# A transformer layer on one core: compress stage moved into the projection's last tile, memory values as the stationary operand, gathered rows turned in four banks

## The chip, the cores and the metric

One core of one Trainium2 chip runs the whole program in one launch; the other cores are idle. The metric is the device time of one execution in microseconds (us). Everything is float32. The program has its weights in DRAM and its tiles in the core's SBUF; products and transposes by TensorE (PE) end in PSUM, which has eight banks of 128 partitions by 512 float32. VectorE (DVE), ScalarE (ACT) and GpSimd (POOL) work beside it, and SyncE (SP) issues most of the transfers. Engines wait for one another on semaphores.

## The reference, cut to what matters

A layer for 1024 tokens (S) of width 1024: projection, two kinds of attention, cross-attention to a memory of 256 tokens, and 32 experts of which each token takes four. Three parts of it are touched.

```python
# compress: blocks of 32 tokens, stride 16 (63 blocks), for k and for v, two groups g
blk = t[:, cmp_idx] + pos_emb[None, None, :, None, :]
hid = jax.nn.gelu(jnp.einsum('bnlgd,ldf->bngf', blk, w1))      # l 32, d 64, f 128
out = jnp.einsum('bngf,fd->bngd', hid, w2)                     # k's is RMS-normed behind it

# memory attention: 4 heads of 64, 256 memory rows
s = jnp.einsum('bqhd,bkhd->bhqk', q, k) * MEM_HD ** -0.5
p = jax.nn.softmax(s, axis=-1)
o = jnp.einsum('bhqk,bkhd->bqhd', p, v).reshape(B, S, 256)
x = x + o @ w_mo

# experts, top 4 of 32
gu  = t[tok] @ w_gate_up[e] + b_gate_up[e]                     # 1024 -> 2048
act = (up + 1.0) * gate * jax.nn.sigmoid(1.702 * gate)         # clamped gate and up
y   = act @ w_down[e] + b_down[e]                              # 1024 -> 1024, times the gate weight
```

## The kernel before, in words

`program` (L1915) runs the stages one after the other, with a barrier of all engines between two: setup, memory, project, compress, attend, mix, experts. Setup writes a table of relative biases; memory computes the keys and values of the 256 memory rows (`kTm` with heads on two row halves, `vmem`).

**Project** (`stage_project`, L208) goes through eight tiles of 128 tokens, written out as a software pipeline: in tile t TensorE does the products `into(t + 1, ...)` of the next tile in pieces, and between them the steps of tile t: `turn_c` (transposes, L451), `up`, `turn_n` (eight transposes: normed queries and keys, and the raw columns that compress needs), `turn_q` (sixteen transposes of 96 columns' worth of heads, L479). In the last tile, t = 7, no next products stand between these steps. ACT and VectorE copy each turned bank to SBUF, and SP stores it to DRAM (`d_qm`, `d_km` at L282 are the last); the compress columns are stored to the SBUF tile `cnT` by a DMA. At SP's top stands the copy of the bias table to `d_bias` (`rev_copied`). In tile 7 SP also issues `load_compress` (L520 to L527), ten loads of `w1`, `w2` and the position embeddings into the place of `w_in`, whose last product is over.

**Compress** (`stage_compress`, L530): TensorE turns the position embeddings (they become 32 more columns of `cnT`), then does the products at L573, 64 for each of k and v and each group, all with 64 rows of contraction, group 0 on row half 0 and group 1 on row half 1, alternating, into a bank each. ACT computes gelu, TensorE the second product, VectorE and ACT the norm of k, TensorE turns k, SP stores `d_ck` and `d_cv` (L558). At its start SP issues `load_first` (L632): the identity, queries, keys and values of the first head pair, the mask strip and `cvalid`.

**Attend** (`stage_attend`, L643) works through 4 head pairs of 32 units; a unit's scores, maximum (L901), exponential (L859, ACT), transposes (L793) and values follow one another over the engines with two units in flight. VectorE waits at its top for POOL's memset of the score tile `sc` (L709) and for `first_in`; SP's first loads are those of the first pair's other tables (L724), and the gates at the end, which VectorE needs at L939.

**Mix** (`stage_mix`, L1047) has eleven steps; in step t TensorE works on tile a = t (output projection), b (memory queries and scores, L1427), c (memory softmax and values, L1414, output product) and d (router, expert biases by the gates, L1439). The list of TensorE's instructions is written out by hand, and so is VectorE's. For tile c: the probabilities `pr` are turned (eight transposes), then each head's values come from two products with the turned probabilities stationary and 64 moving columns of `vmem` (L1414); VectorE scales the result by the softmax sums to `o` (L1306), TensorE turns `o` in two transposes, VectorE copies `oT` (L1325), and the output product follows. For tile d: `gm`, the gate weights by expert, is turned to `gmT` (32 rows), and two products with 512 columns of `bdown` add the biases (L1439).

**Experts** (`stage_experts`, L1455) is a loop of passes, 32 of which do work, each with one expert and up to 256 rows. The pass's number of rows, read from a plan in DRAM, decides through `ARMS` which segments it has: f of 128 rows in four units, h of 64 in two, q of 32, g of 64; "a block" below is segment f. A pass on TensorE: the gate-up products (L1788) unit by unit; the turning of the activations (`turn_act`, L1766); the turning of the *next* pass's gathered rows `xg` (`turn_rows`, L1756 to L1762: four row banks' worth of two columns each, 8 transposes for one block of rows, 16 for two); then the down products (`whole` at L1878, `half` at L1893), in whose second chunk `last_turn` turns the last activations. ACT copies the turned rows, `copy_rows` (L1587) to `xT_e`, and the turned activations (L1607) to `aT`, in one order: the activation copies of this pass come before the row copies. The row banks are two, `ROW_BANK = (7, 5)`, used twice each, so turn k waits for the copy of turn k - 2.

```python
for k in range(4):
    pe.wait_ge(s_xTc, CREDIT + 4 * i + max(k - 1, 0))
    for kk in range(2):
        for b in range(nb):
            c = 2 * k + kk
            mm = pe.transpose(ps[:, ROW_BANK[k % 2], kk * PASS + b * P:kk * PASS + (b + 1) * P], xg[:, b, c * P:(c + 1) * P], ident[:, :])
    mm.then_inc(s_xT, 1)
```

## Time and profile before

| what | value |
|---|---|
| median of 3 runs (lowest, highest) | 3097.82 us (3090.96, 3100.35) |
| the profiled execution's own time | 3101.04 us |
| its span in the trace | 3099.3 us |
| mean granted TensorE clock | 0.944 of full |
| TensorE busy | 2753.2 us (89%), 12040 instructions |
| VectorE, ScalarE, GpSimd busy | 1121.5 (36%), 592.7 (19%), 220.3 (7%) |
| transfers | 570.19 MB, mean 184 GB/s |
| gate-up products (L1788) | 1032.2 us |
| down products (L1878) | 531.6 us |
| one VectorE operation on 128x1024 from PSUM (L1733) | 1.28 us |

In the rows below a group or instruction is named by its engine, its line in the program, its operation and `out<-in` by the names of the tiles; then come shapes and a count. In brackets or behind the last bar stands the idle time of the engine just before it, and behind `<-` what released it (engine, tile, line). "issue" means that nothing the profile shows was waited for. SPq and POOLq are the instructions with which these engines issue transfers. PEclk is the clock that TensorE was granted, as a share of full speed. Stages in this execution: projection to about 350 us, compress to 391, attention to about 880, mix to 1196, experts to the end.

### The profile page before, as it was taken

How to read it: one execution, taken by the hardware profiler on the slowest of the kernel's cores; microseconds unless marked ns; L12 is line 12 of the kernel's file. 1: busy time of each engine (PE TensorE's matmuls, PEld its weight loads, DVE VectorE, ACT ScalarE, POOL GpSimd, SP SyncE). 2: the span in 40 equal slices, each digit the busy share in tenths (PEclk: the TensorE clock that was granted, in tenths of full speed). 3: DMA queues.
4: the chain of work that ended last, by engine and by line, in shares of the span. 5: the costliest groups of instructions: out<-in, count | busy, mean ns of one | idle time of the engine just before them, and what ended most of it. 6: DMA issues, size and time to landing. Idle time of an engine off the chain costs nothing.

```text
span 3099.3 us, 41426 instructions
## 1 busy us (share of the span) xinstructions
PE 2753.2 (89%) x12040; PEld 1369.3 (44%) x12041; DVE 1121.5 (36%) x2925; ACT 592.7 (19%) x1582; POOL 220.3 (7%) x188
## 2 busy tenths in 40 slices
PE   6999589999879984899999899999999999899995
PEld 3555456666545652343444344434333434344332
DVE  2667357767636652223222121221222222122221
ACT  1222145655523320000000000000001000010000
POOL 0000000000001111100000100010110010100110
PEclk9999689999989975899999999999999999999998
DMA  8322562130031205957556777587887677755880
GB/s 291 88 60 61 123 184 53 41 92 15 15 96 48 69 28 213 362 186 261 179 184 226 295 288 271 181 286 266 299 312 254 249 261 248 299 183 182 295 303 14
DMA packets 294613, 570.19 MB, mean 184 GB/s; under 512 B 78734, under 2 KB 117646, under 8 KB 274040
## 3 DMA queue, kind: packets, MB, share of 16 engines
q1 hardware_dynamic: 255661, 530.27, 48.0%
q0 software_dynamic: 21152, 38.52, 5.4%
q10 hardware_dynamic: 17707, 0.22, 0.3%
q8 instruction: 52, 0.85, 0.1%
q14 instruction: 41, 0.34, 0.0%
HBM read 542.65 MB, written 69.88 MB: 198 GB/s over the span
## 4 chain that ended last, share of the span: by engine, by line
PE 49%; DMA 5%; issue 3%; DVE 2%; ACTq 1%; ACT 1%; POOL 0%; POOLq 0%; SPq 0%; DVEq 0%
PE ps L1788 27%; PE ps L1878 17%; DMA out<-ys_e,dst 3%; PE ps L1893 2%; PE ps L1761 1%; DVE gu L1689 1%; DMA xg<-d_h,src 1%; PE ps L1766 1%; DMA wg<-in_w_gate_up 1%; ACT xT_e L1587 1%; ACTq L1502 0%; DVE gg L1692 0%; DVE ys_e L1733 0%; POOL out L1569 0%; DVE ys_e L1731 0%
## 5 line engine op out<-in xcount | busy, mean ns | idle before, releaser
L1788 PE MATMUL ps<-wg,xT_e 128*64 128x512 f32 (+2 forms) x4032 | 1032.2, 599 | 35.9 <-issue 26.5
L1788 PEld LDWEIGHTS ps<-wg,xT_e 128*64 128x64 f32 (+2 forms) x4032 | 390.1, 146 | 647.4 <-issue 647.4
L1878 PE MATMUL ps<-w_rows,aT 128*128 128x512 f32 x1152 | 531.6, 617 | 9.1 <-ACT xT_e L1587 9.1
L1689 DVE TENSOR_TENSOR gu<-ps,bias 64x512 f32<-64x512 f32 (+2 forms) x252 | 173.6, 689 | 587.9 <-PE ps L1788 561.5
L1878 PEld LDWEIGHTS ps<-w_rows,aT 128*128 128x128 f32 x1152 | 222.5, 198 | 273.4 <-issue 271.4
L1629 ACT ACTIVATE ss<-gg 128x256 f32<-128x256 f32 x146 | 60.8, 416 | 1374.6 <-issue 763.3
L1733 DVE TENSOR_SCALAR ys_e<-ps,dst 128x1024 f32<-128x1024 f32 x36 | 46.2, 1284 | 579.8 <-PE ps L1878 579.8
L1569 POOL DMA_INDIRECT out<-ys_e,dst x64 | 101.9, 1592 | 1408.9 <-DVE ys_e L1733 926.2
L442 PE MATMUL ps<-w_in,hT_a 128*128 128x430 f32 x512 | 193.4, 530 | 6.3 <-DVE hT_a L345 6.3
L793 PE MATMUL ps<-ident_t,sc 128*128 128x128 f32 x880 | 151.8, 290 | 29.7 <-ACT sc L859 26.2
L859 ACT ACTIVATE sc<-sc,nm 128x640 f32<-128x640 f32 (+15 forms) x256 | 161.5, 633 | 54.0 <-DVE nm L901 54.0
L1761 PE MATMUL ps<-ident_e,xg 128*128 128x128 f32 x392 | 63.2, 304 | 92.3 <-ACT xT_e L1587 54.7
L793 PEld LDWEIGHTS ps<-ident_t,sc 128*128 128x128 f32 x880 | 97.3, 142 | 90.5 <-ACT sc L859 63.2
L442 PEld LDWEIGHTS ps<-w_in,hT_a 128*128 128x128 f32 x512 | 95.8, 192 | 88.0 <-issue 79.6
L1699 DVE TENSOR_TENSOR aa<-vv,ss 128x256 f32<-128x256 f32 x146 | 62.1, 425 | 155.9 <-ACT ss L1629 145.8
L1362 PE MATMUL ps<-w_rows,yT_x 128*128 128x512 f32 x256 | 114.6, 602 | 1.4 <-DVE yT_x L1218 1.4
L908 DVE COPY pT<-ps 128x512 f32<-128x512 f32 (+3 forms) x176 | 86.0, 488 | 72.8 <-PE ps L793 72.0
L1607 ACT ACTIVATE aT<-ps 128x256 f32<-128x256 f32 x146 | 52.2, 376 | 278.7 <-PE ps L1766 274.2
L852 ACT ACTIVATE pT<-ps 128x512 f32<-128x512 f32 (+3 forms) x176 | 76.2, 433 | 133.8 <-PE ps L793 133.3
L1761 PEld LDWEIGHTS ps<-ident_e,xg 128*128 128x128 f32 x392 | 48.4, 155 | 103.6 <-ACT xT_e L1587 62.7
L1554 POOL DMA_INDIRECT xg<-d_h,src x66 | 68.6, 1039 | 296.0 <-issue 296.0
L1766 PEld LDWEIGHTS ps<-ident_e,aa 128*128 128x128 f32 x292 | 50.6, 200 | 78.3 <-issue 58.7
(293 smaller groups left out, 2473.7 us busy)
## 6 DMA issues: line engine op xcount, KB each, us to landing
wg<-in_w_gate_up SPq DMA_DIRECT2D x128, 2048.0 KB, 9.1
w_rows<-in_w_down SPq DMA_DIRECT2D x128, 1024.0 KB
bias<-in_b_gate_up SPq DMA_DIRECT2D x32, 1024.0 KB, 9.4
d_bias<-d_rev SPq DMA_DIRECT2D x1, 10368.0 KB, 38.1
w_in<-in_w_in SPq DMA_DIRECT2D x1, 6880.0 KB, 24.8
x_a<-in_x POOLq DMA_DIRECT2D x8, 512.0 KB, 4.2
kn<-d_kn SPq DMA_DIRECT2D x8, 512.0 KB
strip_t<-d_bias SPq DMA_DIRECT2D x8, 512.0 KB
```

Of the source, the lines that this page charges most:

```text
L442: mm = pe.matmul(ps[:, 4 * b + c, 0:PCH], hT[b][:, k, :], w_in[:, k, c * PCH:(c + 1) * PCH], start=(k == 0), stop=(k == KD - 1))
L793: mm = pe.transpose(ps[:, 4 + h, (i % 4) * P:(i % 4 + 1) * P], sc[:, u % DEPTH, h, i * P:(i + 1) * P], ident[:, :])
L852: act.activation(dst, src, ACT.Copy).then_inc(s_cp[h], 1)
L859: act.activation(sc[:, k, h, 0:w], sc[:, k, h, 0:w], ACT.Exp, bias=nm[:, k, h, n - 1:n], scale=-1.0, accum_out=rs[:, k, h:h + 1]).then_inc ...
L908: dve.tensor_copy(dst, src).then_inc(s_cp[h], 1)
L1362: mm = pe.matmul(ps[:, bank, 0:cols.stop - cols.start], src[:, k, :], w[:, k, cols], start=(k == 0), stop=(k == n - 1))
L1569: pool.indirect_dma_start(out=e.out[0], out_offset=bass.IndirectOffsetOnAxis(ap=dst[:, b, 0:1], axis=0), in_=ys[:, b, :], in_offset=None, ...
L1689: read = dve.tensor_tensor(gu[part, :], ps[part, BANK[k][j], :], bias[part, cols], ALU.add)
L1761: mm = pe.transpose(ps[:, ROW_BANK[k % 2], kk * PASS + b * P:kk * PASS + (b + 1) * P], xg[:, b, c * P:(c + 1) * P], ident[:, :])
L1766: mm = pe.transpose(ps[:, ACT_BANK[k][j], f * P:(f + 1) * P], aa[:, AA[k][j], f::2], ident[:, :])
L1788: mm = pe.matmul(ps[g * kind:(g + 1) * kind, BANK[k][j], :], xT[:, kk, t0:t0 + kind], wg[:, j * groups + g, kk, :], start=(kk == 0), stop= ...
L1878: mm = pe.matmul(ps[:, 2 + 2 * b + h, :], aT[:, j, b * P:(b + 1) * P], wd[:, c, j % 2, h * 512:(h + 1) * 512], start=(j == 0), stop=(j == ...
```

## The change

Three parts. **Front:** `stage_compress` is gone and its work is in tile 7 of the projection. The position embeddings are loaded at SP's top; `turn_last` turns them and the raw columns straight to a bank that ACT copies to `cnT` (the two transposes in `turn_n` and the store to `cnT` go in this tile); k's 128 products and the first quarter of v's stand before `turn_q`, the rest behind it, with the second products. k's loads and v's have a semaphore each. `load_first` (identity, mask strip, `cvalid`) is issued in tile 1, the first pair's queries, keys and values (`load_first_heads`) at the end of the projection, into the place of the last three of the eight row groups of `w_in`, a tile of its own now. In attention the memset of `sc` is gone, and the first values wait for `first_v_in`. **Mix:** the probabilities are scaled before they are turned, `vmem` is the stationary operand with two heads on two column halves, so that the product comes out turned and `o`, its two transposes and their copy go; the gate weights are doubled, and the two bias products use row groups 0 to 31 and 32 to 63. **Experts:** four row banks, no wait between the turns, the wait for the row copies at other places.

```diff
-N_MEMORY, N_PROJECT = 5, 14
+N_MEMORY, N_PROJECT = 5, 15
...
-    for dst, src in ((e.ident_a[:, :], e.c_ident), (e.w_in_t[:, :, :], e.w_in[0].rearrange("(k p) n -> p k n", p=P)),
+    w_in = e.w_in[0].rearrange("(k p) n -> p k n", p=P)
+    for dst, src in ((e.ident_a[:, :], e.c_ident), (e.w_in_t[:, :, :], w_in[:, 0:KD - 3, :]), (e.w_in_end[:, :, :], w_in[:, KD - 3:, :]),
```

SP in the projection:

```diff
+                    if t == 1:
+                        load_first(nc, e, sp)
                     if t == NT - 1:
                         load_compress(nc, e, sp)
...
+                sp.wait_ge(s_kT, 1)
+                sp.dma_start(e.d_ck.rearrange("g d n -> d g n"), kT[:, :, :]).then_inc(s_out, 16)
+                sp.wait_ge(s_cc, 1)
+                sp.dma_start(e.d_cv.rearrange("g n d -> n g d"), cc[:, G:, :]).then_inc(s_out, 16)
                 for b in range(2):
-                    sp.wait_ge(s_st[b], 160 * (NT // 2))
+                    sp.wait_ge(s_st[b], 160 * (NT // 2) - 16 * b)
+                load_first_heads(e, sp)
+                sp.wait_ge(s_out, 32)
```

TensorE in the projection:

```diff
+                def turn_last():
...
+                    for i in range(2):
+                        at = i * (P + CMP_LEN)
+                        pe.transpose(ps[:, 0, at:at + P], pr[b][:, C_KC + i * P:C_KC + (i + 1) * P], ident[:, :])
+                        mm = pe.transpose(ps[:, 0, at + P:at + P + CMP_LEN], pos[:, i, :, :].rearrange("p g d -> p (g d)"), ident[0:CMP_LEN, 0:CMP_LEN])
+                    mm.then_inc(s_last, 1)
+
+                def products(i, ls):
+                    if ls[0] == 0:
+                        pe.wait_ge(e.cmp_in[i], 16 * N_CMP)
+                        pe.wait_ge(s_cnT, 1)
...
+                    for l in ls:
+                        for g in range(G):
+                            half = slice(g * HD, (g + 1) * HD)
+                            mm = pe.matmul(ps[:, CMP_BANK[i][g], 0:NCMP + 2], w1[half, i, l, :], e.cnT[half, i, l:l + S + 1:CMP_STRIDE],
+                                           start=(l == 0), stop=(l == CMP_LEN - 1))
...
+                    if not more:
+                        turn_last()
                     turn_c(t)
...
+                    else:
+                        products(0, range(CMP_LEN))
+                        products(1, range(CMP_LEN // 4))
                     turn_q(t)
...
+                second(0)
+                products(1, range(CMP_LEN // 4, CMP_LEN))
+                pe.wait_ge(s_ck, 1)
...
+                second(1)
```

Attention:

```diff
-                pool.memset(sc[:, :, :, :], 0.0).then_inc(s_set, 1)
...
+                    if u == 0:
+                        pe.wait_ge(e.first_v_in, 32)
...
-                dve.wait_ge(s_set, 1)
-                dve.wait_ge(e.first_in, 16 * N_FIRST_MLA)
+                dve.wait_ge(e.strip_in, 48)
```

Mix, VectorE:

```diff
+                        wait("p", c, MH)
+                        step(dve.reciprocal(rs[:, c, :], rs[:, c, :]))
+                        dve.tensor_tensor(pr[:, :, :], pr[:, :, :], bcast(rs[:, c, :].unsqueeze(2), [P, MH, N_MEM]), ALU.mult).then_inc(m["pn"], 1)
...
-                        dve.tensor_tensor(o[:, :, :], ps[:, 6, 0:256].rearrange("p (h d) -> p h d", d=MHD),
-                                          bcast(rs[:, c, :].unsqueeze(2), [P, MH, MHD]), ALU.mult).then_inc(m["on"], 1)
+                        dve.tensor_copy(oT[:, :, :], ps[:, 6, 0:256].rearrange("p (j n) -> p j n", n=P)).then_inc(m["oTd"], 1)
```

Mix, TensorE:

```diff
-                        for j in range(2 * MH):
-                            mm = pe.matmul(ps[:, 6, (j // 2) * MHD:(j // 2 + 1) * MHD], pT[:, j, :], e.vmem[:, j % 2, j // 2, :], start=(j % 2 == 0), stop=(j % 2 == 1))
+                        for pair in range(MH // 2):
+                            for k in range(2):
+                                for h in range(2):
+                                    j = 2 * pair + h
+                                    mm = pe.matmul(ps[h * MHD:(h + 1) * MHD, 6, pair * P:(pair + 1) * P], e.vmem[:, k, j, :], pT[:, 2 * j + k, :], start=(k == 0), stop=(k == 1))
...
-                            mm = pe.matmul(ps[:, 2 + c2, :], gmT[:, :], bdown[:, c2 * 512:(c2 + 1) * 512], start=True, stop=True)
+                            r = slice(c2 * NE, (c2 + 1) * NE)
+                            mm = pe.matmul(ps[:, 2 + c2, :], gmT[r, :], bdown[r, :], start=True, stop=True)
```

Experts:

```diff
-        ROW_BANK = (7, 5)
+        ROW_BANK = (7, 4, 5, 0)
...
-                        pe.wait_ge(s_xTc, CREDIT + 4 * i + max(k - 1, 0))
...
+                        pe.wait_ge(s_aTc["g"], CREDIT + 2 * i + 2)
+                        hold(pe, e.pe_passed)
                         with pe.If(after > P):
                             turn_rows(i + 1, 2)
```

`last_turn`, `whole` and `half` of the experts:

```diff
-                            rows_copied(3)
+                            rows_copied(1)
...
                             if b:
-                                rows_copied(4)
-                                copied("g", 2)
+                                rows_copied(3)
                                 copied("h", 1)
                             else:
-                                copied("f", 3)
+                                for k, have in (("q", 1), ("h", 1), ("f", 3)):
+                                    copied(k, have)
...
+                            rows_copied(2)
                             copied(*(("h", 1) if turn else ("q", 1)))
```

## Rows read from the trace of the kernel before

**Rows 1.** Page, the chain that ended last, shares of the span by engine.
```profile
PE 49%; DMA 5%; issue 3%; DVE 2%; ACTq 1%; ACT 1%; POOL 0%; POOLq 0%; SPq 0%; DVEq 0%
```
**Rows 2.** Groups by line, 1200 to 3099 us: busy us, mean ns | idle before.
```profile
L1761 PE MATMUL ps<-ident_e,xg 128*128 128x128 f32 x392 | 63.2, 304 | 92.3 <-ACT xT_e L1587 54.7 <-DMA xg<-d_h,src 37.6
```
**Rows 3.** TensorE in order of time, one pass: start us, us, what, [idle before].
```profile
1709.44 0.60 PE L1761 MATMUL ps<-ident_e,xg 128*128 128x128 f32 x4
1711.82 0.66 PE L1761 MATMUL ps<-ident_e,xg 128*128 128x128 f32 x4 [1.77 <-ACT xT_e L1587]
1712.36 5.39 PE L1878 MATMUL ps<-w_rows,aT 128*128 128x512 f32 x8
```
**Rows 4.** ACT in order of time, same pass.
```profile
1710.55 0.64 ACT L1607 ACTIVATE aT<-ps 128x256 f32<-128x256 f32 x2
```
**Rows 5.** TensorE in order of time, a pass without a block.
```profile
2198.66 6.78 PE L1878 MATMUL ps<-w_rows,aT 128*128 128x512 f32 x8 [1.11 <-ACT xT_e L1587]
```
**Rows 6.** Windows in experts: us, busy of PE PEld DVE ACT POOL, clock, DMA, GB/s.
```profile
1360.50:1364.00 3.50, 3.50 (x10) 1.62 (x9) 0.00 (x0) 0.49 (x2) 0.00 (x0) 1.00 1.05 408
1712.40:1717.60 5.20, 5.20 (x10) 2.17 (x10) 0.00 (x0) 0.45 (x2) 0.00 (x0) 0.67 1.06 422
2198.70:2205.30 6.60, 6.60 (x9) 2.74 (x10) 0.00 (x0) 0.00 (x0) 0.00 (x0) 0.53 1.05 410
```
**Rows 7.** TensorE in order of time, end of projection and compress.
```profile
320.54 0.90 PE L451 MATMUL ps<-ident_a,cn 128*128 128x128 f32 x3 [7.01 <-DVE cn L370]
...
341.32 3.54 PE L479 MATMUL ps<-ident_a,qk 128*96 128x128 f32 x16 [9.91 <-DVE qk L408]
...
356.69 27.57 PE L573 MATMUL ps<-cnT,w_in 64*128 64x65 f32 x256 [0.32 <-DVE cnT L606]
```
**Rows 8.** SP's issues in order of time, 329 to 394 us.
```profile
329.35 4.47 SPq L527 DMA_DIRECT2D w_in<-in_cmp_v_w  x1
...
346.58 0.54 SPq L282 DMA_DIRECT2D d_km<-qkT  x1
...
390.80 0.52 SPq L558 DMA_DIRECT2D d_cv<-cc  x1
...
393.38 0.33 SPq L724 DMA_DIRECT2D qn<-d_qn  x1
```
**Rows 9.** Transfers by issue: KB each, median us from issue to landing.
```profile
d_bias<-d_rev SPq DMA_DIRECT2D x1, 10368.0 KB, 38.1
...
w_in<-in_cmp_v_w SPq DMA_DIRECT2D x1, 32.0 KB, 9.9
```
**Rows 10.** Windows, columns as in rows 6: projection's last tile, compress, mix.
```profile
330.00:332.00 2.00, 1.07 (x8) 0.86 (x8) 1.93 (x4) 0.20 (x1) 0.00 (x0) 1.00 1.22 204
356.70:384.20 27.50, 27.50 (x257) 27.38 (x257) 0.16 (x1) 0.52 (x2) 0.00 (x0) 0.50 0.35 79
1104.00:1119.00 15.00, 9.21 (x65) 8.07 (x63) 11.02 (x26) 4.70 (x8) 0.00 (x0) 1.00 0.18 70
```
**Rows 11.** Attention's start in order of time; last, km's issue to landing.
```profile
393.38 6.92 POOL L709 MEMSET sc<- 128x8192 f32 x1 [117.39 <-POOLq L98]
...
402.36 1.15 ACT L859 ACTIVATE sc<-sc,nm 128x1024 f32<-128x1024 f32 x1 [7.69 <-DVE nm L901]
...
411.25 0.23 DVE L939 TENSOR_SCALAR gates<-gates,cvalid 128x8 f32<-128x8 f32 x1 [2.66 <-DMA gates<-d_gt]
...
DMA to landing us min/median/max: 8.3/8.6/8.8
```
**Rows 12.** Mix: TensorE's groups by line, 1000 to 1100; VectorE in order of time.
```profile
L1439 PE MATMUL ps<-bdown,gmT 32*128 32x512 f32 x15 | 7.4, 608 | 0.0
L1414 PE MATMUL ps<-vmem,pT_x 128*128 128x64 f32 x48 | 5.7, 272 | 0.0
L1427 PE MATMUL ps<-kTm,qT_x 64*128 64x256 f32 x24 | 3.4, 402 | 0.0
...
1020.71 0.19 DVE L1276 TENSOR_TENSOR lg<-ps,rb 128x32 f32<-128x32 f32 x1 [5.57 <-PE ps L1362]
```

More of the change, by code:

```diff
@@ L236, in stage_project @@
         nT = pair("nT", [P, 8, P])
+        pos = sb("pos_c", [CMP_LEN, 2, G, HD])
+        pb = sb("pb", [CMP_HID, 2])
+        hid = sb("hid", [CMP_HID, 2, G * NCMP])
+        cc = sb("cc", [NCMP, 2 * G, HD])
+        sqc = sb("sq_c", [NCMP, G, HD])
+        stc = sb("st_c", [NCMP, G])
+        kT = sb("kT_c", [HD, G, NCMP])
         names = lambda *ns: (e.dma_sem("a_" + n) for n in ns)
@@ L323, in _ @@
                         spread(t + 2)
+                    if t == NT - 1:
+                        act.wait_ge(s_last, 1)
+                        act.activation(e.cnT[:, :, t * P:], ps[:, 0, 0:2 * (P + CMP_LEN)].rearrange("p (i n) -> p i n", i=2), ACT.Copy).then_inc(s_cnT, 1)
                     rest(t)
+                act.wait_ge(s_ssqc, 1)
+                act.activation(stc[:, :], stc[:, :], ACT.Sqrt, bias=eps[0:NCMP, 0:1], scale=1.0 / HD).then_inc(s_stdc, 1)
+                hidden(1)
             @block.vector
```

246 lines of the change are left out of this document (103 added, 143 removed).

## The prediction

> **What bounds the kernel now.** Read the page first: TensorE is busy 89% of the span (the table above), and the chain that ended last is half TensorE, most of it the experts' two lines of products (L1788, L1878) [rows 1]. So I ask where TensorE stands still, and go through the stages in which the change has a part: the experts (1200 to 3099 us), the end of the projection and the compress stage behind it (313 to 411 us), the mix stage (880 to 1196 us).
>
> *Experts.* In the groups of lines, L1761, the turning of the next pass's rows, has the largest idle time before it: 54.7 us until ACT has copied a bank, 37.6 us until a gather lands [rows 2]. The order of time shows the first within one pass: four transposes, 1.77 us idle until ACT's copy of the first row bank, four more, then the down products at once [rows 3]. ACT was late for a second reason: before the row copies it did the activation copies of the same pass, which ended at 1711.19 [rows 4]. Passes without a block of 128 rows also wait 1.11 us for the fourth copy before their down products [rows 5]. And the clock: behind such a gap the first eight down products (3.5 us at full clock) took 5.2 and 6.6 us, at a granted clock of 0.67 and 0.53 [rows 6]. Of the 32 passes, eleven show this: five of 5.3 us, six of 5.4 to 6.8 us, together 24 us over 3.6.
>
> *Projection to attention.* The last tile leaves TensorE idle until 320.5 and from 331.4 to 341.3; behind it the compress stage runs alone: 256 instructions of products in 27.57 us [rows 7]. SP's issues mark the ends: last projection store 346.58, the compress stage's last store 390.80, attention's first load 393.38 [rows 8].
>
> **The change, part by part.** Times are from the profiled execution (span 3099.3, its own time 3101.04, 3.2 above the median 3097.82).
>
> 1. *Rows turned in four banks.* No transpose waits for a copy. With one block of rows the eight take 8 x 0.15 = 1.2 us [rows 3]. The first down products now wait for the activation copies instead (explicit waits for q, h and f): in the pass of [rows 3, 4] start 1711.19 + 0.06, against 1712.36, so 1.1 us saved of 1.77 idle. With two blocks the 16 transposes (2.4 us) are the longer term. Done for every pass by its own rows: 20 passes with a 128-row block save 0.87 to 1.46, 23.1 us; nine without it must still have three row copies, 0.28 us each for one block and 0.55 for two, behind the activation copies, and save 11.3 us; the three small ones save 2.4 us (two of them begin with a late gather). Sum 37 us. The new wait for g's two copies costs at most 0.3 us in the one pass that has g; elsewhere the count is there long before. The last turn's wait is for the row bank it uses and comes 3.5 us later: nothing. The gather chain starts at the end of the previous pass's down products, and the saving lies before that point, so it isn't lost to it.
>    Clock: the stretch without large products shrinks from 3.0 to 1.9 us in block passes and from 5 to about 4 us in the others. I take back the five smaller falls (8.4 us) and 3 us of the 15.7 of the others, since in those the gate-up weights, issued at the end of the units, land only a few us before the next pass. Bounds: 0 and 24 us; taken 11. **Experts 48 us**, bounds 30 and 61.
>
> 2. *Compress in the last tile.* turn_last (four transposes) fits into the idle time before 320.5, and ACT's added copy (some 0.5 us) too: there ACT waits for VectorE as TensorE does. k's products start at 331.4. v's last load was issued at 329.35 and lands 9.9 us later, at 339.3 [rows 8, 9]; the pos loads are gone from between, so no later. 16 pairs of v, 1.7 us, end at 341.0. turn_q at full clock, 16 times 0.15 less overlap, 2.2 us, 343.5; the two evictions and stores follow, 1 us before today's. ACT does k's hidden units in between (2 us with their table load, an estimate), done at 340.7. second(0), 0.7 us, and 48 pairs, 5.2 us: 349.4. Then today's tail without its key half (which runs beside the pairs: root, scale and turning done by 350.2): hidden 0.7, product 0.5, copy 0.3: d_cv issued at 351.3. Four loads of the first heads behind it on SP, 3 us, and 1 us of barrier: attention begins at 355.8 against 393.38, 37.6 us earlier.
>    What is late next: before, scores began at once and VectorE waited for the memset, so that the first exponential stood 9.0 us into the stage [rows 11]. Now km, issued at 352.3, lands 8.6 us later [rows 11], 360.9, and I give scores and maximum 7.1 us (before, both fitted into less than those 9.0): the exponential 12.2 us into the stage. VectorE then stops at the gates, which landed 17.9 us into the stage [rows 11] at the end of SP's first loads; 2 MB of first-head loads lie ahead of them in the same queue, 4 to 8 us at the 200 to 250 GB/s of these stretches, of which 3 are over before the stage. I take 5.3 us given back. **Front 32 us**. The clock is the open term: at 0.50 throughout k ends at 345.2, the 16 pairs at 348.6, turn_q at 352.1, the rest at 362.8, attention at 369.4, which leaves 19 us. I take the full clock, since the nearest row has low work holding it: 15 us of transposes and narrow products, TensorE 61% busy, at 1.00, though the 27.5 us of products never raised it from 0.50 [rows 10]. The memset's 6.92 us are no extra gain: 2.66 of waiting for the gates hid behind them.
>    A rule against the trace: the rows show TensorE busy for all of 27.5 us and the clock at 0.50 to the end. The Trainium skill (TensorE: Matmul & The Clock Gate, "Why this matters for your kernels") says that sustained busy time brings the full rate; by it the old products would have risen too and cost some 15 us, and the gain would be about 13 us smaller. The trace disagrees for these narrow products, and the sum goes by the rows.
>
> 3. *Mix stage*, where TensorE is the bound in the steady tiles: no idle time before its product groups [rows 12]. Per tile: the value products take 0.119 us per instruction [rows 12], 16 of them 1.9; with the 64-column values stationary on two column halves, two at a time, I take 0.055, 0.9. Two transposes go, 0.15 each as in [rows 3], 0.3 us, with the round trip over VectorE. The bias products, 0.49 us each [rows 12], four in a row; kTm's of 256 columns on two row halves take 0.14 each where one after the other would give twice that [rows 12], so the two biases side by side save 0.86. Sum 2.2, less 0.1. Added on VectorE: the scaling of 1024 probabilities (1.28 us for as many columns in the table above) and a copy; it has 5.57 us idle there before the logits [rows 12] and its product is wanted 4 us later: nothing. Eight tiles: **17 us**. Lower bound, if nothing runs side by side: 5; upper 21.
>
> Moving 0.5 MB of strip and two small loads to tile 1 and splitting w_in are hidden: SP awaits d_bias's copy, which is issued before the first tile and lands 38.1 us later [rows 9], before tile 1's stores are due, and what SP stores there is awaited two tiles later.
>
> Sum 48 + 32 + 17 = 97: 3101.0 - 97 = 3004 on the profiled execution, **3001** as a median.
>
> **The rivals.** (a) *Half clock in the products*: for it, they never raised it; against, the 15 us at 1.00. It costs 13 us: 3014. (b) *The experts' wait only changes hands*: ACT's activation copies and row copies set the start of the down products anyway, or the weights, and the clock falls as before. For it, 1.1 saved of 1.77; against, weights issued 20 us ahead in passes with a block. Experts 30: 3019. 
> **How the numbers follow.** What a measurement of this kernel can tell is 0.3%, 9 us. Forecast 0.50, (a) 0.18, (b) 0.16, (c) 0.05, (d) 0.06, (e) 0.03, a race of several small losses that ends within 0.3% 0.02. (a) and (b) together give 3032. Range 2980 to 3035. Faster 0.95, same 0.02, slower 0.03.
>
> **What would show it.** Right: idle before the rows' transposes only from gathers, about 38 us; the first eight down products 3.6 us in nearly all passes; attention's first load near 356; clock 1.00 from 331 to 349; the mix period 2.1 us shorter. Wrong: products at 0.215 a pair, turn_q behind 345; a wait for v's weights of over 1 us; TensorE idle before the down products by more than 0.7 us; the wait for the gates over 6 us.

## The result, and the profile after

The changed kernel takes 3014.05 us (median of 4 runs, 3010.69 to 3017.63) against 3097.72 for the kernel before (4 runs): ratio 0.973, 95% interval 0.9718 to 0.9743, or 84 us less. The forecast was 3001 with a range of 2980 to 3035. On the profiled executions, against which the sum was made, the span goes from 3099.3 to 3012.1: 87.2 us where 97 were forecast.

Five points in the order of time cut the span into stages: the issue of attention's first load, the end of its last value product, the start of the last expert count of mix (L1418), the start of the first gate-up product, the end of the last down product.

| us | before | after | gained | forecast |
|---|---|---|---|---|
| start to attention's first load | 393.4 | 358.5 | 34.9 | 37.6 |
| attention, to its last value product | 451.7 | 459.2 | -7.5 | -5.3 |
| mix, to the last expert count | 336.1 | 320.0 | 16.1 | 17 |
| to the first gate-up product | 41.5 | 43.3 | -1.8 | 0 |
| experts, to the last down product | 1845.1 | 1799.0 | 46.1 | 48 |

This table compares one execution with one. Experiment 1 shows how far each stage moves by itself, and two of these gains change by it: experts (36 us instead of 46) and mix (near 19 instead of 16).

**Experts.** Part 5 of the page after, the groups that answer to [rows 2], and the page before's down products (which had 531.6 busy and 9.1 idle):

```profile
L1798 PE MATMUL ps<-wg,xT_e 128*64 128x512 f32 (+2 forms) x4032 | 1033.3, 601 | 40.6 <-issue 27.9
L1890 PE MATMUL ps<-w_rows,aT 128*128 128x512 f32 x1152 | 515.0, 602 | 31.2 <-ACT xT_e L1598 18.9
L1771 PE MATMUL ps<-ident_e,xg 128*128 128x128 f32 x392 | 53.6, 291 | 42.1 <-DMA xg<-d_h,src 40.3
L1906 PE MATMUL ps<-w_rows,aT 128*64 128x512 f32 x352 | 82.4, 616 | 3.1 <-ACT xT_e L1598 3.1
```

The 54.7 us in which the row transposes waited for ACT are gone; what is left before L1771 are gathers, but for 1.8 us. A part stands before the down products now: 31.2 us, against 9.1. From the end of the last activation transposes to the first down product the 32 passes took 131.1 us in sum before and 95.6 after. TensorE in order of time, a pass with one block of rows and one without a block, and ACT in the first of them:

```profile
2034.18 1.04 PE L1771 MATMUL ps<-ident_e,xg 128*128 128x128 f32 x8
2036.24 1.12 PE L1890 MATMUL ps<-w_rows,aT 128*128 128x512 f32 x2 [1.03 <-ACT aT L1618]
...
2126.53 1.04 PE L1771 MATMUL ps<-ident_e,xg 128*128 128x128 f32 x8
2130.42 5.23 PE L1890 MATMUL ps<-w_rows,aT 128*128 128x512 f32 x8 [2.86 <-ACT xT_e L1598]
```

```profile
2034.97 0.42 ACT L1640 ACTIVATE ss<-gg 128x256 f32<-128x256 f32 x1 [6.41 <-DVE gg L1703]
2035.29 0.64 ACT L1618 ACTIVATE aT<-ps 128x256 f32<-128x256 f32 x2
```

The start of the down products is now ACT's: it does a sigmoid (L1640) before the activation copies and these before the rows. The clock: the first eight down products took 3.5 us (from the first to the next other instruction) in nearly every pass, and over 5 in 4 of them (11 before), 118.1 us in sum against 136.2. The four are all passes without a block, and the length of the stretch does not tell which: with 4.12 and with 4.32 us between the last activation transposes and the down products, one pass of each had the fall and another had not.

**Front.** TensorE in order of time after (L562 are the compress products, L538 is `turn_q`, L570 the second products, L790 attention's first scores), and windows as in [rows 6, 10]:

```profile
329.19 7.50 PE L562 MATMUL ps<-cnT,w_in 64*128 64x65 f32 x128
338.61 3.68 PE L562 MATMUL ps<-cnT,w_in 64*128 64x65 f32 x32 [1.91 <-DMA w_in<-in_cmp_v_w]
342.22 3.27 PE L538 MATMUL ps<-ident_a,qk 128*96 128x128 f32 x16
345.41 0.44 PE L570 MATMUL ps<-w_in,hid 128*63 128x64 f32 x4
345.79 5.69 PE L562 MATMUL ps<-cnT,w_in 64*128 64x65 f32 x96
...
363.82 7.03 PE L790 MATMUL ps<-w_in_end 96*128 96x512 f32 x12 [11.10 <-DMA w_in_end<-d_km]
```

```profile
329.20:336.60 7.40, 7.40 (x129) 7.30 (x128) 6.89 (x6) 2.51 (x4) 0.00 (x0) 1.00 1.23 212
338.70:342.20 3.50, 3.50 (x32) 3.40 (x32) 0.64 (x2) 0.04 (x1) 0.00 (x0) 0.50 0.30 76
345.80:351.20 5.40, 5.40 (x97) 5.40 (x97) 2.42 (x7) 3.60 (x4) 0.00 (x0) 1.00 0.56 144
363.80:370.80 7.00, 6.97 (x12) 3.13 (x12) 2.93 (x9) 0.84 (x1) 0.00 (x0) 0.64 0.99 242
```

k's 128 instructions ran at full clock, 0.117 us a pair; the 27.57 us of [rows 7] have become 16.87, and of these only a part is not hidden. v's first quarter waited 1.91 us for its load and then ran at 0.50, and `turn_q` behind it took 3.27 us. SP's issues after, and VectorE at the gates:

```profile
353.07 0.27 SPq L303 DMA_DIRECT2D d_cv<-cc  x1
...
358.51 4.55 SPq L735 DMA_DIRECT2D qn<-d_qn  x1
...
375.11 0.41 SPq L745 DMA_DIRECT2D gates<-d_gt  x1
```

```profile
380.92 0.23 DVE L951 TENSOR_SCALAR gates<-gates,cvalid 128x8 f32<-128x8 f32 x1 [5.65 <-DMA gates<-d_gt]
```

VectorE works on the gates 22.4 us into the stage; before it was 17.9 [rows 11].

**Mix.** Groups of lines with shapes apart, TensorE, before (880 to 1180 us) and then after (852 to 1137 us); both windows hold 28 of the 32 bias instructions:

```profile
L1362 PE MATMUL ps<-w_mo,oT_x 128*128 128x512 f32 x64 | 34.2, 684 | 1.9 <-DVE oT_x L1325 1.5
L1414 PE MATMUL ps<-vmem,pT_x 128*128 128x64 f32 x128 | 17.7, 299 | 3.9 <-DVE pT_x L1217 3.9
L1439 PE MATMUL ps<-bdown,gmT 32*128 32x512 f32 x28 | 17.4, 751 | 0.4 <-DVE gmT L1312 0.4
L1432 PE MATMUL ps<-ident_x,o_x 128*128 128x128 f32 x16 | 4.0, 335 | 0.0
```

```profile
L1429 PE MATMUL ps<-pT_x,vmem 128*64 128x128 f32 x128 | 10.5, 316 | 2.7 <-DVE pT_x L1229 2.7
L1450 PE MATMUL ps<-bdown,gmT 32*128 32x512 f32 x28 | 9.8, 782 | 0.8 <-DVE gmT L1327 0.8
```

Both pairs run side by side: 17.7 us of value products became 10.5, and 17.4 us of bias products 9.8.

### The profile page after: what moved, and what is told of

It is laid out like the page before. It is cut to its first block, busy times and chain, and to the rows that moved or that the text cites. A ratio compares the mean times of both kernels' runs of the same rounds, so it can differ in the third digit from the quotient of the medians.

```text
span 3012.1 us, 41358 instructions
## 1 busy us (share of the span) xinstructions
PE 2702.6 (90%) x12024; PEld 1344.0 (45%) x12025; DVE 1129.3 (37%) x2931; ACT 589.9 (20%) x1585; POOL 219.0 (7%) x187
## 4 chain that ended last, share of the span: by engine, by line
PE 47%; DMA 7%; issue 3%; DVE 2%; ACTq 1%; ACT 1%; POOL 0%; POOLq 0%; SPq 0%; DVEq 0%
PE ps L1798 26%; PE ps L1890 16%; DMA out<-ys_e,dst 4%; PE ps L1906 2%; DMA xg<-d_h,src 1%; DMA wg<-in_w_gate_up 1%; PE ps L1771 1%; PE ps L1776 1%; DVE gu L1700 1%; ACTq L1513 0%; DVE ys_e L1744 0%; POOL out L1580 0%; ACT aT L1618 0%; DVE gg L1703 0%; DVE ys_e L1742 0%
## 5 line engine op out<-in xcount | busy, mean ns | idle before, releaser
L1798 PE MATMUL ps<-wg,xT_e 128*64 128x512 f32 (+2 forms) x4032 | 1033.3, 601 | 40.6 <-issue 27.9
L1890 PE MATMUL ps<-w_rows,aT 128*128 128x512 f32 x1152 | 515.0, 602 | 31.2 <-ACT xT_e L1598 18.9
L1640 ACT ACTIVATE ss<-gg 128x256 f32<-128x256 f32 x146 | 60.8, 417 | 1383.6 <-issue 775.4
L804 PE MATMUL ps<-ident_t,sc 128*128 128x128 f32 x880 | 151.6, 289 | 30.1 <-ACT sc L872 26.7
L501 PE MATMUL ps<-w_in,hT_a 128*128 128x430 f32 x320 | 128.1, 538 | 6.3 <-DVE hT_a L386 6.3
L865 ACT ACTIVATE pT<-ps 128x512 f32<-128x512 f32 (+3 forms) x176 | 76.1, 433 | 135.0 <-PE ps L804 134.5
L1771 PE MATMUL ps<-ident_e,xg 128*128 128x128 f32 x392 | 53.6, 291 | 42.1 <-DMA xg<-d_h,src 40.3
L1906 PE MATMUL ps<-w_rows,aT 128*64 128x512 f32 x352 | 82.4, 616 | 3.1 <-ACT xT_e L1598 3.1
L501 PEld LDWEIGHTS ps<-w_in,hT_a 128*128 128x128 f32 x320 | 59.9, 195 | 54.7 <-issue 46.4
```

The lines of the kernel that those rows point to most:

```text
L501: mm = pe.matmul(ps[:, 4 * b + c, 0:PCH], hT[b][:, k, :], w_in_rows(k)[:, c * PCH:(c + 1) * PCH], start=(k == 0), stop=(k == KD - 1))
L804: mm = pe.transpose(ps[:, 4 + h, (i % 4) * P:(i % 4 + 1) * P], sc[:, u % DEPTH, h, i * P:(i + 1) * P], ident[:, :])
L1771: mm = pe.transpose(ps[:, ROW_BANK[k], kk * PASS + b * P:kk * PASS + (b + 1) * P], xg[:, b, c * P:(c + 1) * P], ident[:, :])
L1798: mm = pe.matmul(ps[g * kind:(g + 1) * kind, BANK[k][j], :], xT[:, kk, t0:t0 + kind], wg[:, j * groups + g, kk, :], start=(kk == 0), stop= ...
L1890: mm = pe.matmul(ps[:, 2 + 2 * b + h, :], aT[:, j, b * P:(b + 1) * P], wd[:, c, j % 2, h * 512:(h + 1) * 512], start=(j == 0), stop=(j == ...
L1906: mm = pe.matmul(ps[h * r:(h + 1) * r, 4, :], aT[:, j, t0:t0 + r], wd[:, c, j % 2, h * 512:(h + 1) * 512], start=(j == 0), stop=(j == JD - 1))
```

## The experiments

Twelve kernels. Each ratio is to the kernel before, run beside it; a median is compared with the changed kernel's 3014.05 us where the edit is on the changed kernel.

**1. The parts alone.** Each is the kernel before with one part of the diff shown above, cut at the stages.

> The kernel before with the experts' part alone. Theory: the three parts are separate stages and add up, so this one brings what the experts' stage gained between the two traces, 46 us (35.5 of waits before the down products, some 17 of clock, 6 given back to the gate-up weights): about 3051 us, ratio 0.985. Rival (it only pays in a kernel in which the stages before are also shorter, or weights and gathers take it back): under 30 us, 3068 or more. Rival (two thirds of the whole gain is here): 60 us or more, 3038.

> The kernel before with the mix part alone. Theory: TensorE is the bound of that stage, 16.2 us between the traces (about 2.1 per step): 3081.5 us, ratio 0.9948. Rival (the shorter products only expose VectorE, the gain between the traces came from another alignment): under 8 us. The 1.5 us that the experts' start lost would be seen here too, if it belongs to this part.

> The kernel before with the front part alone. Theory: attention's first load stands 35 us earlier, of which attention's start gives back 7.5 (gates later in the queue, half clock behind the idle time): 27.5 us, 3070 us, ratio 0.991. My forecast had 32 (3066). Rival (the memset that is gone hides more, or the barrier is shorter): over 32.

Measured: experts 3060.40, ratio 0.9876 (0.986 to 0.9891), some 38 us; mix 3077.11, 0.9927 (0.9912 to 0.9941), 23 us; front 3071.11, 0.9908 (0.9893 to 0.9922), 28 us. The sum is 89, and together they bring 84, within what these intervals allow: the parts add up. The stages in the traces, us:

| kernel | to attention's first load | attention | mix | granted clock in mix | experts |
|---|---|---|---|---|---|
| before | 393.4 | 451.7 | 336.1 | 0.888 | 1845.1 |
| experts alone | 391.0 | 452.4 | 338.8 | 0.878 | 1808.4 |
| mix alone | 391.0 | 452.4 | 320.1 | 0.876 | 1843.3 |
| front alone | 356.9 | 458.2 | 338.7 | 0.878 | 1838.1 |
| all | 358.5 | 459.2 | 320.0 | 0.876 | 1799.0 |

How far a stage moves by itself is seen where a kernel does not touch it. The old experts' stage stands in five traces (before, mix alone, front alone and the two of experiment 2): 1829.1 to 1845.1 us, 1839.4 on average. The new one stands unchanged in five (experts alone, all, experiments 6, 7 and 8): 1799.0 to 1810.8, 1803.4 on average. So the part is worth some 36 us in the traces and 38 in the runs; the 46 between the two profiled executions of the table above came from a long one before and a short one after. The averages of the terms: from activation transposes to down products 130.4 us before and 95.9 after; first eight down products 135.0 and 121.3 (9 to 12 falls, then 4 to 7); waits for gate-up weights 6.9 and 12.6; waits of the activation transposes for VectorE 10.8 and 14.3.

Mix moves with the granted clock. At nearly the same clock the part is worth 18.7 us (338.8 against 320.1); the 336.1 of the kernel before was an execution with a higher clock in that stage.

**2. Mix in halves**, on the kernel before. Values alone is the mix part with these lines, and the tiles `gm` and `gmT` that belong to them, put back; bias alone is the kernel before with these lines the other way, the gate weights doubled.

```diff
-bdown = sb("bdown", [2 * NE, D // 2])
+bdown = sb("bdown", [NE, D])
...
-                            r = slice(c2 * NE, (c2 + 1) * NE)
-                            mm = pe.matmul(ps[:, 2 + c2, :], gmT[r, :], bdown[r, :], start=True, stop=True)
+                            mm = pe.matmul(ps[:, 2 + c2, :], gmT[:, :], bdown[:, c2 * 512:(c2 + 1) * 512], start=True, stop=True)
```

> The kernel before with the values part of the mix change alone (probabilities scaled first, values stationary on two column halves, no turning of o). Theory: my forecast's terms, 1.0 for the products and 0.3 for the transposes a tile, less what VectorE's scaling adds: mix stage about 10 us shorter (336 to 326), 8 tiles. Rival (the scaling of 1024 columns, 1.22 us, delays the transposes of the probabilities and takes part of it back): 6 or less.

> The kernel before with the bias part alone (gate weights doubled, two products on two row groups). Theory: the two run side by side, 1.0 us saved a tile less the copy: mix stage 6 to 8 us shorter. Rival (they run one after the other, or the copy on VectorE sits on the path): under 3 us. Values and bias together should make the 16 to 17 us that the mix part makes alone.

Values alone: 3086.91, ratio 0.997 (0.9955 to 0.9984), stage 325.7 at a granted clock of 0.885, so 10.4 us shorter than the 336.1 at 0.888, as expected. Bias alone: 3093.27, 0.9985 (0.9975 to 0.9995), stage 336.3 at a granted clock of 0.876, so 2.5 us less than the 338.8 of the kernels with the old mix at nearly that clock (0.878), where 6 to 8 were expected; the runs differ by 3.4. Yet its products did halve. Groups of lines, bias alone:

```profile
L1363 PE MATMUL ps<-w_mo,oT_x 128*128 128x512 f32 x64 | 33.8, 677 | 6.2 <-DVE oT_x L1326 6.2
L1441 PE MATMUL ps<-bdown,gmT 32*128 32x512 f32 x28 | 9.8, 781 | 0.4 <-DVE gmT L1313 0.4
```

In TensorE's list the bias products stand between the turning of `o` and the output product, which waits for VectorE's copy `oT`. They covered that copy; made short, they expose it: 6.2 us of waiting, 1.9 before. Over the stage TensorE is busy 7.2 us less than with the old mix in those kernels (278.4 against 285.6) and idle 5.2 us more (58.1 against 52.9). Once the values part has taken `o`'s turning away, the bias part brings 7.5 us: 325.7 with values alone at a clock of 0.885, and 318.2 with the whole part at 0.886 (experiments 6 and 8).

**3. All row copies awaited** before the down products, on the changed kernel.

```diff
+                            rows_copied(4)
                             if b:
-                                rows_copied(3)
...
-                            rows_copied(2)
+                            rows_copied(4)
```

> The changed kernel, but the down products wait for all four row copies in every pass. The idle time before the down products grows: with a block of rows by the copies behind the activation copies, 1.0 us (one block) or 2.0 us (two blocks) in some 21 passes, by 0.2 to 0.5 in nine others: waits 30 to 35 us. Theory of the clock (it falls where the stretch without large products is over some 3.5 us, as in the 11 passes before): stretches grow to 3 to 4 us, so some of the 27 passes that hold it now lose it, 1.7 us each: 3014 + 33 + 5 to 25 = 3050 to 3070. Rival (the clock follows something else than that stretch, and does not fall): 3045. Rival (the waits are covered by the gate-up weights, which land later anyway): under 3035.

Measured 3074.46, ratio 0.9923 (0.9904 to 0.9942), 60 us slower than the change, and the experts' stage is 1859.9 us, longer than before the change. From the activation transposes to the down products 139.6 us (44 more than with the change), and 17 passes with a clock fall instead of 4, 142.0 us for the first eight products (24 more). Both terms of the theory were right in kind and low in size: the stretch grew by more than the 30 to 35 us expected, the clock took the top of 5 to 25, and the time lies above 3050 to 3070. But the length that the expectation names for a fall is not in the rows. Counted from the last gate-up product to the first down product, five of the eleven falls before stood behind 3.2 to 3.3 us, and eight passes with 3.7 to 4.2 us had none; here, of two passes with 3.67 us one fell. What decides in one pass stays open.

```profile
L1890 PE MATMUL ps<-w_rows,aT 128*128 128x512 f32 x1152 | 536.9, 622 | 68.6 <-ACT xT_e L1598 68.6
```

**4. Wide products in the wait**, on the changed kernel.

```diff
                             whole(0, ("f", 3))
                         with pe.Else():
+                            for _ in range(3):
+                                pe.matmul(ps[:, 6, :], ident[:, :], wide[:, :], start=True, stop=True)
```

`wide` is a tile of zeros, set by POOL at the start of the stage.

> The changed kernel with three products of 512 columns (six instructions, 2.6 us at full clock) between the turned rows and the down products in the nine passes without a block, where TensorE waits 2.0 to 2.9 us for the row copies. What they compute is not used, and the wait itself stays. Theory of the clock (it falls because nothing large runs in that stretch, whatever the reason): the four falls among these passes go, up to 7 us of the experts' stage, and waits are unchanged within 3 us: stage 1792 to 1797 against 1799. Rival (the fall comes from the transposes or from the transfers then running, not from the missing products): four or more falls stay, and the stage is the same or longer.

Measured 3018.57, ratio 0.9748 (0.973 to 0.9765). No fall is left, the first eight products take 107.6 us in sum against 118.1. In order of time, the pass that is shown above:

```profile
2127.53 1.04 PE L1774 MATMUL ps<-ident_e,xg 128*128 128x128 f32 x8
2128.40 2.74 PE L1918 MATMUL ps<-wide,ident_e 128*128 128x512 f32 x6
2131.42 3.70 PE L1894 MATMUL ps<-w_rows,aT 128*128 128x512 f32 x8 [0.27 <-ACT xT_e L1601]
```

From the last row transpose to the down products it is 2.85 us as before, and the eight products take 3.70 instead of 5.23. So the fall comes from the stretch without large products, not from the transposes or the transfers beside it. The runs do not tell this kernel from the changed one. Its stage is 8 us longer in the trace (1807.2), where 2 to 7 less was expected. The stretches before the down products add 13 us, partly in two of the three small passes, where the products had no wait to fill, and the clock gives 10.5 back; gate-up weights are waited for 18.9 us instead of 11.2. The untouched stage moves by 12 us, so the 8 are not told from nothing, but a gain is not there either.

**5. ACT's order**, on the changed kernel.

```diff
                                 for j in range(4):
+                                    if j == 3:
+                                        copy_act(i, "f", 2)
                                     sigmoid("f", j)
-                                    if j:
+                                    if j in (1, 2):
                                         copy_act(i, "f", j - 1)
...
                             with act.Else():
                                 none("f")
...
+                                sigmoid("h", 0)
+                                with act.If(hasq > 0):
+                                    copy_act(i, "q", 0)
                                 copy_act(i, "h", 0)
...
+                                next_rows(i + 1, after)
+                                sigmoid("h", 1)
                                 copy_act(i, "h", 1)
```

> The changed kernel with another order on ACT: with a block of rows, the copy of the block's third turned activation comes before the sigmoid of its fourth; without a block, the activation copies and the row copies come before the sigmoid of h's second half. Theory (ACT's order sets the start of the down products, and the clock goes with the length of the stretch without large products): some 15 waits of 1.0 us before the down products go and nine of 2.4 to 2.9 shrink to under 0.7, together 30 us, and the four clock falls go, 7 us; the gate-up weights take back 6 to 12: 3014 - 28 = 2986. Rival (the gate-up weights and the gathers, not ACT, set the pass's length from here on): under 10 us gained, 3005 or more, with the waits moved before the gate-up products. Rival (the sigmoid that is now late holds up the last turned activation by as much): TensorE waits before the last turn of a pass, and nothing is gained.

Measured 2992.99, ratio 0.9659 (0.964 to 0.9677), 21 us faster than the change. Its experts, two of the groups of lines from 1175 to 3060:

```profile
L1901 PE MATMUL ps<-w_rows,aT 128*128 128x512 f32 x1152 | 507.4, 595 | 13.9 <-ACT aT L1618 7.9 <-ACT xT_e L1598 6.0
L1809 PE MATMUL ps<-wg,xT_e 128*32 128x512 f32 x1280 | 150.7, 625 | 33.7 <-DMA wg<-in_w_gate_up 31.9 <-issue 1.8
```

Down to 68.9 us between activation transposes and down products (26.7 less), no clock fall, 8.4 us less for the first products. And the rival's part: the wait for gate-up weights is 31.9 us in the passes' narrow segment, 11.2 with the change and 7.5 before. The gate-up products themselves take 10.5 us longer (1043.8 against 1033.3). Of some 35 us won before and in the down products the stage keeps 12 in this trace (1787.0), which is the slowest of its five runs; the medians keep 21. The weights' wait is the same in the second kernel with this order (32.6 us, experiment 9). What the next step meets are the weights.

**6. The gates first**, on the changed kernel: their load moved from the end of SP's first tables to the front.

```diff
-                    if hp == 0:
-                        sp.dma_start(gates[:, :, :, :], e.d_gt.rearrange("(t p) (h b) -> p t h b", p=P, b=3)).then_inc(s_gate, 16)
...
+                sp.dma_start(gates[:, :, :, :], e.d_gt.rearrange("(t p) (h b) -> p t h b", p=P, b=3)).then_inc(s_gate, 16)
                 load_nsa(0)
                 load_mla(1)
```

> The changed kernel with the load of the gates as the first of attention's loads. Theory: VectorE's wait of 5.65 us for them goes, and attention's give-back of 7.5 us against the kernel before shrinks to about 3: 3014 - 4 = 3010. Rival (the rest of the first tables, or the scores at half clock, are as late): less than 1.5 us. Below what the runs can tell; the stage's length in the trace decides it.

Measured 3007.77, ratio 0.9717 (0.9695 to 0.974): the intervals overlap with the change's, so the trace decides. VectorE no longer waits at the gates. From the stage's first load (356.9) to its last value product it takes 451.1 us, 8.1 less than with the change, twice the 4 expected, and as long as before. In six traces with the changed attention as it is the stage takes 456.8 to 460.1, so the 8 stand clear of its own movement: the give-back of 7.5 hung on this one load.

**7. Wide products before the first scores**, on the changed kernel.

```diff
                 pe.wait_ge(e.strip_in, 48)
+                for _ in range(20):
+                    pe.matmul(ps[:, 5, :], ident[:, :], mstrip[:, 0:512], start=True, stop=True)
                 scores(0)
```

> The changed kernel with 20 products of 512 columns into an unused bank at the start of attention, while TensorE waits for the first queries and keys. What it computes is not used. Theory (the idle time of 11 us is why the first twelve scores run at a granted clock of 0.64 and 7.0 us instead of some 4.7): clock 1.00 from the first score, the first exponential 2 to 3 us earlier, attention 2 to 4 us shorter: 3011. Rival (the gates' wait swallows what the scores gain): attention's length unchanged within 1 us. Rival (the products last longer than the wait for the keys): some us slower.

Measured 3019.68, ratio 0.9747 (0.9727 to 0.9767). The intervals of this kernel and the changed one overlap. The products ran 19.2 us (two instructions each; I had reckoned with one) and ended some 12 us after the scores had begun with the change. Their windows, and the scores behind them:

```profile
350.00:356.70 6.70, 0.45 (x5) 0.34 (x5) 0.28 (x1) 0.34 (x3) 0.00 (x0) 0.76 0.66 161
356.70:359.00 2.30, 2.30 (x3) 1.14 (x4) 0.00 (x0) 1.24 (x1) 0.00 (x0) 0.50 1.01 227
359.00:362.00 3.00, 3.00 (x6) 1.14 (x5) 0.00 (x0) 0.00 (x0) 0.00 (x0) 0.78 1.32 202
362.00:366.00 4.00, 4.00 (x11) 1.84 (x10) 0.00 (x0) 0.00 (x0) 0.00 (x0) 1.00 1.05 250
...
375.80:380.00 4.20, 4.20 (x13) 2.02 (x11) 2.79 (x7) 0.69 (x1) 0.00 (x0) 1.00 1.04 226
```

At full clock the twelve score instructions take 4.46 us, not 7.03. They began 11.9 us later than with the change, and VectorE came to the gates 3.6 us later (384.54 against 380.92) without a wait: 11.9 less the 2.6 of clock and less the 5.65 of waiting. So the scores had room up to the gates' wait. The stage is 462.1 us long, 2.9 more than with the change, where 2 to 4 less was expected.

**8. k's products wait for v's load too**, on the changed kernel.

```diff
-                        pe.wait_ge(e.cmp_in[i], 16 * N_CMP)
+                        pe.wait_ge(e.cmp_in[0], 16 * N_CMP)
+                        pe.wait_ge(e.cmp_in[1], 16 * N_CMP)
```

> The changed kernel, but k's products too wait for v's loads. Theory: k's 128 products start when v's load lands, 338.6 instead of 329.2, v's first quarter and the turning of the last queries move by the 9.4 us less the 1.9 us that they wait today, and attention's first load comes 7.5 us later, 3021. Rival (the end of the stage hangs on ACT's and VectorE's tail of the projection, so that k's products have slack): under 3 us, 3016. If the clock falls in the longer idle time (half clock in the products): 7 us more.

Measured 3024.93, ratio 0.9765 (0.9744 to 0.9787), 11 us slower than the change. In order of time, then windows on these products, on `turn_q` and on the rest of v's products:

```profile
338.00 17.33 PE L563 MATMUL ps<-cnT,w_in 64*128 64x65 f32 x160 [7.28 <-issue]
```

```profile
341.00:355.00 14.00, 14.00 (x136) 14.00 (x134) 0.00 (x0) 1.97 (x4) 0.00 (x0) 0.50 0.01 1
355.30:358.30 3.00, 3.00 (x17) 2.78 (x16) 0.00 (x0) 0.00 (x0) 0.00 (x0) 0.58 0.00 0
358.80:364.00 5.20, 5.20 (x93) 5.20 (x94) 2.37 (x7) 3.56 (x4) 0.00 (x0) 1.00 0.57 145
```

Attention's first load stands at 370.8, 12.3 us later. Behind 7.28 us of idle time the products ran at half clock to their end, 0.217 us a pair: the forecast's rival (a), made to happen by one wait. The separate waits are worth 12 us in the trace and 11 in the runs, more by the clock (some 8 us for these 160 instructions) than by the start.

**9. Together**: ACT's order, the gates first, and five wide products before the scores (ten instructions).

> The changed kernel with the other order on ACT, the gates loaded first, and five products of 512 columns (10 instructions, some 6.5 us with the clock rising) ahead of attention's first scores. Theory (separate stages, gains add): experts' stage 1787 us as with the order alone, attention 8 to 10 us shorter by the gates and 1 to 3 by the clock: 2993 - 10 = 2983, ratio 0.963. Rival (with the gates first, the first loads end later and the products only push the scores back): 2990 or more.

Measured 2987.84, ratio 0.9647 (0.9628 to 0.9667): 26 us below the changed kernel and 109 below the one before, the fastest here. Most of it is ACT's order; the interval does not tell it from that kernel alone, but the trace does: attention ends its value products at 808.2, against 816.7 there. The scores run at a granted clock of 1.00 and take 4.46 us, the first exponential stands 9.9 us into the stage instead of 11.7 with the gates alone, and the stage is 449.7 us long against 451.1. That is the 1 to 3 us expected of the wide products, but no more than the stage moves by itself, so it is not shown.

## Why the prediction was right, and by how much its terms were off

**Rows turned in four banks.** The waits: 35.5 us of the 37 forecast between the two profiled executions, 34.5 in the averages of experiment 1, by the mechanism named, the start passing to ACT's activation copies. The clock: 18.1 us between the two, 13.7 on average, against 11 taken. So both terms held, 48 us together, and the stage still gained 36 and not 48. The step that was mis-sized is what takes back, named in rival (b) and put at nothing in the sum: the gate-up weights 5.7 us and the waits for VectorE's last activations 3.5, with some 3 us unexplained. That the table shows 46 beside the forecast's 48 is luck of the two executions. The 36 lie nearer to the 30 us of rival (b), the experts' wait only changes hands, than to 48; what it said of the clock was wrong, what it said of the weights was right in part. ACT's order was worth 21 us on top (experiment 5), so its mechanism was the next one. Rival (e), clock lost in every pass, was wrong for 28 of 32; experiment 3 shows that it was not far: with 44 us more before the down products, 17 passes fall. Two of the signs named for being wrong did appear without making it so: 1.91 us of waiting for v's weights, and 31.2 us before the down products, 0.97 a pass.

**Compress in the last tile.** The start was right to 2.7 us: 358.5 against 355.8. k began 2.2 us earlier than forecast (329.2) and ended 1.6 earlier. The step that failed is "16 pairs of v, 1.7 us": v's load landed at 338.6 where 339.3 was worked out, but the quarter took 3.68 us. Eight executions have this code with separate waits, and the quarter's time goes with the wait before it:

| wait, us | 0.34 | 0.93 | 1.09 | 1.14 | 1.53 | 1.68 | 1.72 | 1.91 |
|---|---|---|---|---|---|---|---|---|
| quarter, us | 2.06 | 2.20 | 2.41 | 2.56 | 2.97 | 3.68 | 3.68 | 3.68 |

The second step is `turn_q` "at full clock, 2.2 us": it took 3.27, and that is not the wait's doing. In all nine executions it took 3.00 to 3.65 us, also where v's quarter had full clock (experiment 7, TensorE in order of time):

```profile
337.70 2.06 PE L562 MATMUL ps<-cnT,w_in 64*128 64x65 f32 x32 [0.34 <-DMA w_in<-in_cmp_v_w]
340.06 3.48 PE L538 MATMUL ps<-ident_a,qk 128*96 128x128 f32 x16 [0.30 <-DVE qk L449]
```

Why the clock is low there stays open. From `d_cv` to attention's first load went 5.4 us, where I had 4.5. Full clock in k's products was the right choice of the two: experiment 8 shows the other. The give-back was 7.5, not 5.3; "the exponential at 12.2 us" was measured at 11.5, and the gates were late by 4.5 us in the stage. One reckoning in it was wrong: 2 MB at 200 to 250 GB/s are 8 to 10 us, not 4 to 8. Experiment 6 shows that the gates were all of the give-back, within what the stage moves by itself. The scores' clock, which I had not named, cost nothing beside them.

The row and the rule: the Trainium skill (TensorE: Matmul & The Clock Gate, "Why this matters for your kernels") has it that sustained busy time brings the full rate. Experiment 8's 14 us of narrow products at 0.50 and TensorE busy throughout disagree as the rows before did, while the wide products of experiment 7 had the full clock within some 5 us. For the full-rate stretches at k's products both fit.

**Mix.** 16.1 of 17 us between the two executions, 18.7 at nearly the same clock, and the values' half 10.4, as its terms gave. But the bias products' "0.86 a tile" was right only in company: the step "so the two biases side by side save 0.86" took their time as path, when with the old turning of `o` it was cover for VectorE's copy of `oT`. Rival (c), no pairs, was wrong: both pairs show in the busy times.

**Sum.** By the runs, the parts are worth 38 us (experts), 28 (front) and 23 (mix) against 48, 32 and 17: two terms were too large and one too small, so that their errors partly cancel. Of the 10 us missing on the profiled execution, 4.9 are the front's (2.7 the start, 2.2 the give-back), 0.9 mix, 1.8 the start of the experts, 1.9 the experts and 0.6 the tail behind their last product. The last four are not told from nothing: the start of the experts takes 38 to 43 us in the fourteen traces, with no order by kernel. The median then lay 13 us above the forecast, as the profiled execution before had been 3.3 us above its median, and the one after was on its own (3013.81 against 3014.05).

## What to carry to other kernels

When waits on an engine go, look at what that engine's list does next in the producer: here ACT's order of a sigmoid and two copies was worth another 21 us, for no new resource. Before shortening an operation on a full engine, ask whether something waits behind it that it was covering: the bias pairs gained 2.5 us in the old mix and 7.5 once the turned copy beside them was gone. A first load that is issued last is cheap to find: one small table at the end of a queue cost 8 us. And before a stage's gain is read from one trace of each kernel, look at how far that stage moves in kernels that leave it alone, and at its granted clock: here 16 us of 1840 for the experts.

## What the runs showed of the hardware beyond that

- The granted clock was 0.50 in the narrow products behind idle times of 1.91 and 7.28 us and 0.64 on average in the scores behind 11.10 us; behind 0.34 us the narrow products ran at 1.00. What raised it again depended on the work: 14 us of unbroken products with 64 rows and 65 columns did not (0.50), the 16 transposes of 128 columns behind them ran at 0.58 and the same narrow products then at 1.00, and wide products had 1.00 within some 5 us.
- The fall is worth some 1.7 us for the first eight down products (5.23 against 3.53). It came behind a stretch of transposes and idle time in some passes and not in others with the same stretch, and wide products put into that idle time prevented it in each of the 12 passes where they ran.
- SP's first issue of the attention stage took 0.33 us before [rows 8]. With the first pair's loads just ahead of it in the queue it took 4.55 us, and when the gates stood first it was they that took it:

```profile
356.87 4.60 SPq L752 DMA_DIRECT2D gates<-d_gt  x1
361.51 2.82 SPq L735 DMA_DIRECT2D qn<-d_qn  x1
```
